# An SSM projection whose weights' low parts move to GpSimd, with a third place for the weights, a softplus without a reciprocal, and three units multiplied together at its start

## What is computed

```python
def ssm_project(u, w_in, conv_w, conv_b, dt_bias):
    z, xbc, dt = jnp.split(u @ w_in, [D_INNER, D_INNER + CONV_DIM], axis=-1)
    xbc = jax.nn.silu(centred_depthwise_conv(xbc, conv_w, conv_b))
    xs, Bm, Cm = jnp.split(xbc, [D_INNER, D_INNER + SSM_GROUPS_2 * D_STATE], axis=-1)
    dt = jax.nn.softplus(dt.reshape(b, L, 2, SSM_HEADS).astype(F32) + dt_bias.astype(F32))
```

## Time and profile before

| | |
|---|---|
| runs | 1605.48, 1607.57, 1609.26 us |
| median | 1607.57 us |
| the profiled execution, its own time | 1605.15 us |
| its span, first to last instruction | 1603.4 us |
| mean granted TensorE clock | 0.965 |
| TensorE busy (weight loads) | 1498.5 us, 93% (1266.3 us, 79%) |
| DVE, ScalarE, GpSimd busy | 756.5, 598.1, 207.2 us |
| chain that ended last: TensorE, DVE, ScalarE, DMA | 83%, 8%, 4%, 3% |
| moved by DMA | 206.84 MB, 129 GB/s on the mean |
| matmuls of ssm_dt and ssm_in | 1176, from 983.5 to 1208.1 us |

### The profile page before, as it was taken

How to read it: one execution, slowest core, us unless ns; L and a number is a source line. 1 busy time by engine, 2 the same in 40 slices (tenths; PEclk the granted TensorE clock), 3 DMA queues, 4 the chain that set the end, 5 groups by cost and what they waited for, 6 DMA issues and landing times.

```text
span 1603.4 us, 22715 instructions
## 1 busy us (share of the span) xinstructions
PE 1498.5 (93%) x9413; PEld 1266.3 (79%) x9424; DVE 756.5 (47%) x1233; ACT 598.1 (37%) x1126; POOL 207.2 (13%) x195
## 2 busy tenths in 40 slices
PE   7899999989989898999999997799999999999997
PEld 6878789767845586888888885678997788899997
DVE  6762155333258745223222324776745762254453
ACT  4443154144338635222122214432443560343342
POOL 2000186002000021110011110000000120021111
PEclk9799999889989999999999998999999999999998
DMA  7413454676200034223222321232351332645550
GB/s 234 153 54 105 178 209 152 250 323 248 105 1 1 27 105 161 102 74 132 97 87 80 109 86 58 105 106 90 139 183 37 134 131 104 264 165 196 178 171 28
DMA packets 36109, 206.84 MB, mean 129 GB/s; under 512 B 4952, under 2 KB 9480, under 8 KB 14888
## 3 DMA queue, kind: packets, MB, share of 16 engines
q1 hardware_dynamic: 33344, 200.11, 34.7%
q10 hardware_dynamic: 1848, 2.52, 0.9%
q0 software_dynamic: 816, 2.78, 0.5%
HBM read 202.76 MB, written 2.62 MB: 128 GB/s over the span
## 4 chain that ended last, share of the span: by engine, by line
PE 83%; DVE 8%; ACT 4%; DMA 3%; issue 1%; POOL 1%; SPq 1%; ACTq 0%; DVEq 0%; POOLq 0%
PE lin L1729 17%; PE lin L1731 17%; PE lin L1730 17%; PE lin L1696 8%; PE lin L1841 3%; PE modp L1767 2%; DMA ring<-ada_in 2%; PE lin L2295 1%; PE aux L1783 1%; PE lin L2112 1%; PE lin L1712 1%; PE aux L2212 1%; PE lin L1713 1%; PE lin L1714 1%; PE aux L1868 1%
## 5 line engine op out<-in xcount | busy, mean ns | idle before, releaser
L602 DVE TENSOR_TENSOR w_split<-ring,w_split 128x1024 fp32r<-128x1024 f32 (+1 forms) x140 | 187.9, 1347 | 357.4 <-ACT w_split L597 357.0
L597 ACT ACTIVATE w_split<-ring 128x1024 fp32r<-128x1024 f32 (+1 forms) x140 | 158.0, 1132 | 408.8 <-PE lin L1731 362.8
L1729 PE MATMUL lin<-hn_hi,w_split 128*128 128x512 f32 (+1 forms) x768 | 264.9, 345 | 3.5 <-DVE w_split L602 3.5
L1731 PE MATMUL lin<-hn_hi,w_split 128*128 128x512 f32 (+1 forms) x768 | 264.7, 345 | 0.0
L1730 PE MATMUL lin<-hn_lo,w_split 128*128 128x512 f32 (+1 forms) x728 | 249.2, 342 | 0.0
L1729 PEld LDWEIGHTS lin<-hn_hi,w_split 128*128 128x128 f32 x768 | 146.3, 190 | 20.5 <-issue 3.6
L1731 PEld LDWEIGHTS lin<-hn_hi,w_split 128*128 128x128 f32 x768 | 146.3, 191 | 17.2
L1730 PEld LDWEIGHTS lin<-hn_lo,w_split 128*128 128x128 f32 x728 | 138.7, 191 | 15.6
L1729 PE MATMUL lin<-hn_hi,w_split_ssm 128*128 128x512 f32 (+2 forms) x392 | 134.3, 343 | 17.3 <-DVE w_split_ssm L602 11.0
L1730 PE MATMUL lin<-hid_split,w_split 128*128 128x512 f32 (+1 forms) x392 | 133.8, 341 | 0.0
L1731 PE MATMUL lin<-hn_hi,w_split_ssm 128*128 128x512 f32 (+2 forms) x392 | 133.4, 340 | 0.0
(11 more groups left out here) (400 smaller groups left out, 2720.9 us busy)
## 6 DMA issues: line engine op xcount, KB each, us to landing
ring<-ada_in SPq DMA_DIRECT2D x48, 1024.0 KB, 5.0
ring<-ssm_in_in SPq DMA_DIRECT2D x24, 1024.0 KB, 4.9
ring<-od_in_in SPq DMA_DIRECT2D x12, 1024.0 KB, 4.8
ring<-ffn0a_in_in SPq DMA_DIRECT2D x11, 1024.0 KB, 4.8
ring<-ffn0b_in_in SPq DMA_DIRECT2D x11, 1024.0 KB, 4.8
ring<-ffn1a_in_in SPq DMA_DIRECT2D x11, 1024.0 KB, 5.1
ring<-ffn1b_in_in SPq DMA_DIRECT2D x11, 1024.0 KB, 4.8
ring<-ev_in_in SPq DMA_DIRECT2D x9, 1024.0 KB, 13.2
```

Of the source, the lines that this page charges most:

```text
L597: act.activation(parts[:, 0], w, ACT.Copy).then_inc(sig("w_high"), 1)
L602: dve.tensor_tensor(parts[:, 1], w, parts[:, 0].bitcast(F32), ALU.subtract).then_inc(sig("w_low"), 1)
L1729: mm(lin[0:m, tile % RING, 0:width], hi, x_hi, start=kt == 0, stop=False)
L1731: ins = mm(lin[0:m, tile % RING, 0:width], lo, x_hi, start=False, stop=kt == kts - 1)
```

## The change

- `w_split_ssm` gets a third place, in another part of SBUF, so that the high part of unit n + 4 (before, n + 3) stands in ScalarE's loop, and units 1, 2 and 3 are made ahead of it, unit 1 already before the norm's square root.
- GpSimd makes the low parts of units 3 to 31. DVE keeps ssm_dt, 0, 1, 2 and 32 to 47, and waits before 32 until GpSimd's are made. Unit 1's is made between the norm's reciprocal and its first product (`meanwhile`).
- TensorE takes ssm_dt, unit 0 and unit 1 together, tile by tile of the activations, and goes on with unit 2.
- The softplus needs e / (1 + e) with e = exp(-|x|). Before, it is the reciprocal of 1 + e times a difference. Now ScalarE makes exp(-ln(1 + e)) with one more Exp (`dt_share`), and DVE multiplies with that.
- DVE does the convolutions of tiles 0 and 1 while it would wait for `dt_exp`, ahead of the softplus and not behind it.

```diff
--- before.py
+++ after.py
@@ -238,7 +238,9 @@
         od_lo = hn_lo[:, :, L:2 * L]
         _, rows_split, heads_split = places(
             ("rows_start", [P, 27648], F32), ("rows_split", [P, 2, L], F32R), ("heads_split", [P, 2 * M_HEADS], F32R))
-        _, w_split_ssm = places(("ssm_start", [P, 18432], F32), ("w_split_ssm", [P, 2, 2, KT * P], F32R))
+        _, ssm_places = places(("ssm_start", [P, 18432], F32), ("w_split_ssm", [P, 2, 2, KT * P], F32R))
+        _, ssm_place = places(("place_start", [P, 28352], F32), ("w_split_ssm_late", [P, 2, KT * P], F32R))
+        w_split_ssm = (ssm_places[:, 0], ssm_places[:, 1], ssm_place)
         whole_arena = sb("whole_arena", [P, ARENA + HN])
         lin = ctx.enter_context(nc.psum_tensor("lin", [P, RING, 2 * L], F32))
         aux = ctx.enter_context(nc.psum_tensor("aux", [P, AUX, 2 * L], F32))
@@ -405,6 +407,7 @@
         tot = stat_ssm[0:64, 0:2]
         tot_chunk, tot_pick = (small[0:64].rearrange("p a b -> p (a b)")[:, at:at + 2] for at in (48, 52))
         chunk_cols = (slice(0, P), slice(P, L))
+        dt_share = cb[0:64].rearrange("p a b -> p (a b)")
         a_neg = stat_ssm[0:64, 2:3]
 
 
@@ -571,7 +574,7 @@
 
 
             if name[:3] == "ssm":
-                return "ssm_dt", w_split_ssm, 2, 0
+                return "ssm_dt", w_split_ssm, 3, 0
             if name[:4] == "ffn1":
                 return "ffn1a_in", w_split, W_UNITS, 0
             if name == "od_in":
@@ -584,7 +587,8 @@
             per_block = dict(SPLIT)[name] // n
             b, cols = blocks_of[name][u // per_block], cols // per_block
             first, memory, places_, shift = chain(name)
-            parts = memory[:, (unit_of[name] + u - unit_of[first] + shift) % places_, :, 0:cols]
+            place = (unit_of[name] + u - unit_of[first] + shift) % places_
+            parts = memory[place][:, :, 0:cols] if first == "ssm_dt" else memory[:, place, :, 0:cols]
             return parts, ring[:, b % RING, u % per_block * cols:(u % per_block + 1) * cols], b
 
         def weights_hi(act, name, u):
@@ -635,6 +639,9 @@
             taken(pool, "lin", lin_of["ffn0b_out"] + KT - 1)
             for dst, name in ((conv_w, "conv_w"), (ssm_mask, "ssm_mask")):
                 pool.dma_start(dst, t[name]).then_inc(sig("ssm_in"), 16)
+            pool.wait_ge(sig("w_low"), unit_of["ssm_in"] + 3)
+            for u in range(3, 32):
+                weights_lo(pool, "ssm_in", u)
             for n in range(DT_):
                 taken(pool, "lin", y_tile(n))
                 nc.gpsimd.tensor_tensor(ys[:, n], ys[:, n], zs[:, n], ALU.mult).then_inc(sig("y_gated"), 1)
@@ -813,19 +820,21 @@
                 full(act, "lin", lin_of["ffn0b_out"] + KT - 1)
                 weights_hi(act, "ssm_dt", 0)
                 weights_hi(act, "ssm_in", 0)
+                weights_hi(act, "ssm_in", 1)
 
             act_norm(act, 4, 2 * L, "ffn0b_out", (1, 0, 2), True, first_weights)
-            weights_hi(act, "ssm_in", 1)
             weights_hi(act, "ssm_in", 2)
+            weights_hi(act, "ssm_in", 3)
 
             act.wait_ge(sig("dt_abs"), 1)
             own.link(act.activation(dt_tmp, dt_tmp, ACT.Exp, scale=-1.0))
-            own.mark(act.activation(dt_tmp2, dt_tmp, ACT.Ln, bias=ones[0:64, 0:1]))
+            own.link(act.activation(dt_tmp2, dt_tmp, ACT.Ln, bias=ones[0:64, 0:1]))
+            act.activation(dt_share, dt_tmp2, ACT.Exp, scale=-1.0)
             act.activation(a_neg, dt_cols[:, 1:2], ACT.Exp).then_inc(sig("dt_exp"), 1)
             for n in range(48):
                 tile = lin_of["ssm_in"] + n
-                if n + 3 < 48:
-                    weights_hi(act, "ssm_in", n + 3)
+                if n + 4 < 48:
+                    weights_hi(act, "ssm_in", n + 4)
                 if n == 3:
                     act.wait_ge(sig("dt_summed"), 1)
                     act.activation(since_rows, rows_g[0:64], ACT.Exp)
@@ -900,7 +909,7 @@
             act_norm(act, 6, L, "ffn1b_out")
 
 
-        def normed(dve, k, width, a, shifted=False, split=None):
+        def normed(dve, k, width, a, shifted=False, split=None, meanwhile=None):
 
 
             def low(kt):
@@ -911,6 +920,8 @@
             tile = aux_of[f"norm{k}"]
             taken(dve, "aux", tile)
             dve.reciprocal(rcol[:, 0:width // P], rcol[:, 0:width // P]).then_inc(sig("rms"), 1)
+            if meanwhile is not None:
+                meanwhile()
             full(dve, "aux", tile + 1)
             for kt in range(KT):
                 for s in range(width // L):
@@ -986,12 +997,12 @@
             for n in range(RING):
                 taken(dve, "lin", lin_of[name] + KT - 1 - n)
 
-        def modulated(dve, own, k, width, layer, chunk, split=None):
+        def modulated(dve, own, k, width, layer, chunk, split=None, meanwhile=None):
 
             own.link(dve.scalar_tensor_tensor(
                 out=a_col[:], in0=mod[:, layer, (chunk + 1) * KT:(chunk + 2) * KT, :], scalar=1.0,
                 in1=each(g2[:, k - 2, :], 2), op0=ALU.add, op1=ALU.mult))
-            normed(dve, k, width, lambda kt, s: a_col[:, kt, s:s + 1], True, split)
+            normed(dve, k, width, lambda kt, s: a_col[:, kt, s:s + 1], True, split, meanwhile)
 
         def ffn_vector(dve, n, width):
 
@@ -1141,14 +1152,16 @@
 
             weights_lo(dve, "ssm_dt", 0)
             weights_lo(dve, "ssm_in", 0)
-            modulated(dve, own, 4, 2 * L, 1, 0, 2)
-            weights_lo(dve, "ssm_in", 1)
+            modulated(dve, own, 4, 2 * L, 1, 0, 2, lambda: weights_lo(dve, "ssm_in", 1))
+            weights_lo(dve, "ssm_in", 2)
             tile = lin_of["ssm_dt"]
             full(dve, "lin", tile)
             frees(ts(dt2, lin[0:64, tile % RING, :], dt_cols[:, 0:1], None, ALU.add), "lin", tile)
             taken(dve, "lin", tile)
             stt(out=dt_tmp, in0=dt2, scalar=-1.0, in1=dt2, op0=ALU.mult, op1=ALU.max).then_inc(sig("dt_abs"), 1)
-            weights_lo(dve, "ssm_in", 2)
+            dve.wait_ge(sig("ssm_in"), 32)
+            convolve(dve, own, 0)
+            convolve(dve, own, 1)
 
             dve.wait_ge(sig("dt_exp"), 1)
             own.mark(ts(dt2, dt2, 0.0, None, ALU.max))
@@ -1156,14 +1169,9 @@
             own.mark(tt(dt2, dt2, dt_tmp2, ALU.add))
             own.link(ts(dt_tmp3, da, 1.0, None, ALU.subtract))
             own.link(tt(dt_tmp, dt_tmp, dt_tmp3, ALU.subtract))
-            weights_lo(dve, "ssm_in", 3)
-            own.link(dve.reciprocal(da, da))
-            own.link(tt(da, da, dt_tmp, ALU.mult))
+            own.link(tt(da, dt_share, dt_tmp, ALU.mult))
             own.link(tt(dt2, dt2, da, ALU.add))
             own.link(ts(da, dt2, a_neg, -1.0, ALU.mult, ALU.mult))
-            dve.wait_ge(sig("ssm_in"), 32)
-            convolve(dve, own, 0)
-            convolve(dve, own, 1)
 
             one = ones[0:64, 0:1].to_broadcast([64, L])
             for cols in chunk_cols:
@@ -1179,10 +1187,13 @@
             own.mark(tt(rows_g[back], rows_g[back], da[back, 0:L], ALU.add))
             own.mark(ts(log_rows, dt2[:, 0:L], 1e-37, None, ALU.max))
             tt(dt_tmp[back, L:2 * L], dt_tmp[back, L:2 * L], da[back, L:2 * L], ALU.add).then_inc(sig("dt_summed"), 1)
-            for n in range(2, 46):
-                weights_lo(dve, "ssm_in", n + 2)
+            for n in range(2, 44):
                 if n < 32:
                     convolve(dve, own, n)
+                if n + 4 == 32:
+                    dve.wait_ge(sig("w_low"), unit_of["ssm_in"] + 32)
+                if n + 4 >= 32:
+                    weights_lo(dve, "ssm_in", n + 4)
                 if n == 4:
                     dve.wait_ge(sig("dt_weights"), 1)
                     for n_ in range(2):
@@ -2173,10 +2184,10 @@
             feed_forward(0, 3, 2 * L)
             ada(2)
             norm(4, 2 * L)
-            split_unit("ssm_dt", 0, KT, lambda kt: (hn_hi[:, kt, :], hn_lo[:, kt, :]), 2 * L, 2 * M_HEADS,
-                       ("hn_ready", KT * 4))
-
-            for tile in range(48):
+            split_together([("ssm_dt", 0, 2 * M_HEADS), ("ssm_in", 0, P), ("ssm_in", 1, P)],
+                           lambda kt: (hn_hi[:, kt, :], hn_lo[:, kt, :]), 2 * L, KT * 4)
+
+            for tile in range(2, 48):
                 width = 2 * L if tile < 24 else L
                 split_unit("ssm_in", tile, KT, lambda kt: (hn_hi[:, kt, 0:width], hn_lo[:, kt, 0:width]), width)
             pe.wait_ge(sig("dt_rows"), 1)
```

## The result

The changed kernel takes 1596.99 us (median of seven, 1594.90 to 1601.41), the kernel before in the same runs 1606.40 (1602.26 to 1609.26). The ratio is 0.994 with a 95% interval of 0.9924 to 0.9956: some 9.6 us less, and 9.4 between the two medians.

A forecast was written before the change was run, and what follows sets the result against it. TensorE was taken to bound the kernel (83% of the last chain). 15.4 us less without further stops, minus 6.45 for late units and 1.4 for slow matmuls, gave 7.5 less: 1600.0 us, range 1590.5 to 1605.

The forecast's parts named there:

- the stop ahead of unit 2: TensorE, behind the first 72 matmuls: unit 2's high part waits for ssm_dt's last matmul, a new stop of 1.4 us.
- unit 4 late by: TensorE at unit 4: its low part is there at 1015.7, wanted at 1014.9, 0.85 us late.
- unit 6 late by: TensorE at unit 6: tile 2's bank is free at 1029.75, wanted at 1026.6, 3.15 us late.
- unit 8 late by: TensorE at unit 8: high part behind ScalarE's exps, GpSimd's low part ready at 1042.9, wanted at 1040.6, 2.3 us late.
- unit 9 late by: TensorE at unit 9: waits for its bank, 0.15 us late.
- low clock behind the stops: TensorE behind unit 6's stop of 3.15 us: slow matmuls cost 1.4 us, with 0 and 2.8 as ends.
- the norm's delay: ScalarE makes unit 1's high part before its square root, so the norm and the first matmul come 1.04 us later.
- the three units together: Stage start: ssm_dt, units 0 and 1 as 72 matmuls take 18.06 us; unit 2 starts 2.3 us ahead of before.
- A: Softplus on DVE: the chain slips past GpSimd, little is given back, 12 to 15.4 us less; chance 0.27.
- B: Softplus on DVE: held longer, by more table loads, low clock or GpSimd passes, 1603.7 to 1606.1 us; chance 0.15.
- C: Stage start: all 72 matmuls stay at the low clock, 12.7 us more, 1612.8 us; chance 0.08 with its like.
- D: GpSimd's share and third place bring nothing; reciprocal, moved rest and joined units give 6.8 us; inside the forecast's 0.50.

The follow-up runs named there:

- all three steps: Changed kernel plus two GpSimd waits (unit 3 for dt_abs, unit 6 for dt_summed) and ScalarE's high part 8 ahead of the rows' exps: ratio 0.9888, stage 208.56 us.

## Why the prediction was right

The changed kernel was forecast at 1600.0 us with 1590.5 to 1605 as the range, and 7.5 us less; measured are 1597.0 and 9.4 less between the medians (of the 3.0 us by which 1597.0 lies below the forecast, 1.2 are the kernel before, 1606.4 in these runs and 1607.6 in those forecast from). Point by point, with the clock of the stage (us behind its first matmul):

| step | forecast | measured |
|---|---|---|
| start to unit 2: 72 matmuls, low clock, stop | 19.4 | 19.37 |
| of it the stop ahead of unit 2 | 1.4 | 1.18 idle, 1.34 from when it was due |
| unit 4 late by | 0.85 | 0.65 |
| unit 6 late by | 3.15 | 2.51 |
| unit 8 late by | 2.3 | 2.12 |
| unit 9 late by | 0.15 | no idle row |
| low clock behind the stops | 1.4 | nothing beyond unit 8's 2.12 |
| stage | 216.1 | 213.7 |
| stage without any stop behind unit 2 | 208.2 | 208.6 (all three steps) |

(The forecast's 208.2 is 1192.8 less 984.57; 216.1 adds the 6.45 and 1.4. "Late by" is against a pace of 5.44 us a unit from the unit before that was late.)

**Right: what bounds the stage and where the gain comes from.** Both long stops of rows 2 went, and the pace between stops is that of rows 1 and 2: 156.4 us from unit 8 to the end, where 16 wide and 24 narrow units make 156.2.

**Right: what is given back, by the port.** Rows 7 and 8 showed the hold with a copy and with subtractions in other stages; carried over to the softplus they gave the late units 4 and 6 with their releasers, and with ScalarE's order unit 8. The two waits and the reordered instruction took away what each was said to cause. The Trainium skill, SBUF — State Buffer, section "Who interferes with whom", has the same rule, and the trace after bears out both halves of it: 2.79 us for a two-input product of 0.68, 0.75 for a convolution step with its PSUM input.

**Mis-sized: the clock term.** The prediction took 1.4 us for slow matmuls behind the stop ahead of unit 6. They came in one profiled execution and not in the other, and cost nothing in either, because the next unit that waits, unit 8, waits for ScalarE's order. This is the larger of the terms that make the forecast too small. It isn't free everywhere: behind the longer stop of the kernel with the reciprocal 0.4 us of it stayed.

**Mis-sized: unit 6, by 0.6 us.** The forecast had one DVE instruction between the subtractions of units 4 and 5 and none between those of 5 and 6, with 6.6 us of DVE's work left when the last of them ends, 36.1 us behind the first matmul. It does end there (1026.56), but DVE has 5.7 left (the sums end at 1032.26), because the product L1171, 0.7, got in between the two. The bank of unit 6 is free 0.9 earlier for it, and the unit is due 0.25 earlier. Why DVE got in there is open.

**Right, but hidden: the norm's delay.** Forecast 1.04 us; between the two profiles it is 0.18 (10.48 from the last addition to the first matmul before, 10.66 after). The kernel before was profiled while the norm's broadcast ran mostly at the low clock (1.89 us for its eight matmuls, granted 0.55; 1.18 and 0.88 after). Like with like: with unit 1's high part ahead of the root it takes 11.52 or 11.53 where the broadcast is slow (2.05 us, three of the kernels above), 1.04 more than before, and 10.60 to 10.71 where it is fast, against 9.72 or 9.73 without that part: 0.9 to 1.0. The pair of profiles hid some 0.8 of it.

**Half wrong: the three units together.** They were booked as 2.3 us of gain ahead of a sum in which the stops stood as costs of their own. The stops were in fact theirs: ssm_dt alone has none and is 2.0 us faster: 3.4 us of start are given for 5.3 of late units. The prediction's sum counted both and so was right in total; that this part of the change lost time as it stood, it did not see.

**The rivals.** A (GpSimd slips past, 12 to 15.4 less) fell: four DVE instructions were held. One did get in between two subtractions, worth 0.7. B (held longer) didn't come. C (low clock through all 72) fell: seven matmuls at the low clock, about nine in other executions. (The prediction read twelve of them in the stage before; there are ten, from 983.53 to 988.23. Only C and the 0.9 us of a longer low clock use that number.) D (GpSimd and the third place bring nothing) fell: without GpSimd's share the stage is 218.7.

**Where the 11.1 us of the stage are.** Not a sum of parts: the softplus alone 1.8, GpSimd alone minus 5.0, all but GpSimd 6.0, all but the three together 13.1, all but the missing reciprocal 9.4. GpSimd's share needs the third place, by the narrow stops of the run without it. The three together paid only where GpSimd was kept out of the softplus's way. The third place alone on the kernel before wasn't run.

## What to carry to other kernels

Before work is moved to GpSimd, list what DVE does beside it: instructions with two SBUF inputs, and copies and scalar forms within SBUF, stood still here beside GpSimd's subtractions (2.2 to 2.8 us each for 0.2 to 0.7), while those that read PSUM, and a reciprocal with one SBUF input, went on. If such a chain decides when something starts, give GpSimd a wait that keeps its instructions off the chain wherever their own deadline allows it; here two waits and one reordered instruction took another 5 us off the stage. A helper engine that is slower (2.4 us a subtraction, 1.23 on DVE) can need a buffer more: the same share of GpSimd's was worth 5 us in the changed kernel with three places and cost 5 us on the kernel before with two.

## What the runs showed of the hardware that was not expected

- A DVE instruction that waits for the port can be passed over by a whole row of GpSimd's: 12.57 us as a copy, 12.64 as a two-input maximum, seven subtractions each time. In the softplus of the changed kernel one DVE instruction did get in between two subtractions (L1171, which ends at 1024.29 between the two of 1021.35 to 1026.56), and in the kernel with GpSimd alone so did the first of two 64x128 scans, which ends at 1025.69 between the two subtractions of 1023.05 to 1027.84. What decides this was not settled; the operation alone is not it, since the maximum and L1171 are both two-input forms.
- After the same stop of 2.25 us TensorE's next matmuls were slow in one execution (seven, some 0.43 apart, granted clock 0.50) and not in another (0.23 apart, 1.00).
